# How much of the last output products is done tile by tile at the end of four feed-forward layers

## The reference

```python
# gated layers, D_FF = 2816, each with an RMS norm ahead of it and one behind it
g, u = split(rms_norm(x) @ w_in);  h = (silu(g) * u) @ w_out
x = x + 0.5 * rms_norm(h, gain)
# squared-ReLU layers, 4096 hidden features, layer norm behind them
y = square(relu(h @ w_up)) @ w_down
x = layer_norm(alpha * x + (1 + gate) * y)
```

## Time and profile before

| | us |
|---|---|
| median of 3 runs (lowest to highest) | 1333.25 (1332.56 to 1333.79) |
| profiled execution, its own time | 1337.71 |
| its span, first to last instruction | 1335.9 |
| PE busy | 1248.5 (93%) |
| DVE busy | 967.7 (72%) |
| ACT busy | 613.6 (46%) |
| DMA, mean over the span | 205 GB/s |

### The profile page before, as it was taken

One profiled execution on the slowest core, in us unless ns is written; L12 is line 12 of the kernel. 1 busy time (PEld: TensorE's weight loads), 2 busy tenths in 40 slices (PEclk: granted clock), 3 DMA queues, 4 the chain that ended last, 5 costly groups with the idle time before them and its releaser, 6 DMA issues.

```text
span 1335.9 us, 14591 instructions
## 1 busy us (share of the span) xinstructions
PE 1248.5 (93%) x5776; PEld 1021.0 (76%) x5776; DVE 967.7 (72%) x1318; ACT 613.6 (46%) x799; POOL 92.8 (7%) x136
## 2 busy tenths in 40 slices
PE   5999999999999989999999888999979986899996
PEld 4878778888888868787787676888767764788885
DVE  4998868866566788877776469887768876765555
ACT  5544435545663634343555534443434642643430
POOL 2000220003300000000000000000000000000000
PEclk9999999999999989999999989999989987999998
DMA  9988984545545588894473237787824531456540
GB/s 291 327 292 295 321 278 170 177 158 152 161 146 189 195 291 293 308 312 158 139 266 124 97 126 264 272 296 270 299 95 161 194 103 35 161 192 227 189 157 32
DMA packets 132883, 274.30 MB, mean 205 GB/s; under 512 B 6208, under 2 KB 51472, under 8 KB 132816
## 3 DMA queue, kind: packets, MB, share of 16 engines
q1 hardware_dynamic: 114960, 209.80, 46.5%
q0 software_dynamic: 17792, 63.56, 14.1%
q10 hardware_dynamic: 64, 0.02, 0.0%
HBM read 270.41 MB, written 2.93 MB: 205 GB/s over the span
## 4 chain that ended last, share of the span: by engine, by line
PE 71%; DVE 14%; DMA 6%; ACT 5%; issue 3%; SPq 1%; DVEq 0%; ACTq 0%
PE ps L424 22%; PE ps L426 21%; PE ps L425 21%; DVE lo_w L1214 4%; DMA w_raw<-in_ffn_w_in 4%; PE ps L527 3%; ACT hi_w L872 2%; DVE piece_acc L1393 2%; SPq L324 1%; ACT area L1145 1%; DMA w_raw<-in_mlp_w_down 1%; PE ps L496 1%; DVE area L1714 1%; ACT aux L894 1%; PE ps L660 1%
## 5 line engine op out<-in xcount | busy, mean ns | idle before, releaser
L1214 DVE TENSOR_TENSOR lo_w<-w_raw,hi_w 128x2048 fp32r<-128x2048 f32 x198 | 452.2, 2293 | 180.9 <-ACT hi_w L872 180.6
L872 ACT ACTIVATE hi_w<-w_raw 128x2048 fp32r<-128x2048 f32 x198 | 377.7, 1917 | 241.2 <-DMA w_raw<-in_ffn_w_in 88.1
L424 PE MATMUL ps<-hi_w,xT_hi 128*128 128x512 f32 x1120 | 451.5, 403 | 17.9 <-DVE xT_lo L1235 13.6
L426 PE MATMUL ps<-lo_w,xT_hi 128*128 128x512 f32 x1120 | 441.8, 394 | 0.0
L425 PE MATMUL ps<-hi_w,xT_lo 128*128 128x512 f32 x1120 | 441.6, 394 | 0.0
L424 PEld LDWEIGHTS ps<-hi_w,xT_hi 128*128 128x128 f32 x1120 | 213.8, 191 | 65.5 <-issue 22.4
L426 PEld LDWEIGHTS ps<-lo_w,xT_hi 128*128 128x128 f32 x1120 | 213.5, 191 | 46.5
L425 PEld LDWEIGHTS ps<-hi_w,xT_lo 128*128 128x128 f32 x1120 | 213.9, 191 | 42.4
L424 PE MATMUL ps<-hi_w,hT_hi 128*128 128x512 f32 x464 | 186.6, 402 | 19.5 <-DVE hT_lo L1379 19.3
L426 PE MATMUL ps<-lo_w,hT_hi 128*128 128x512 f32 x464 | 183.8, 396 | 0.0
L425 PE MATMUL ps<-hi_w,hT_lo 128*128 128x512 f32 x464 | 183.6, 396 | 0.0
(11 more groups left out here) (215 smaller groups left out, 884.2 us busy)
## 6 DMA issues: line engine op xcount, KB each, us to landing
w_raw<-in_ffn_w_in SPq DMA_DIRECT2D x88, 512.0 KB
aux<-in_ada_w POOLq DMA_DIRECT2D x32, 1024.0 KB, 7.7
w_raw<-in_mlp_w_up SPq DMA_DIRECT2D x32, 1024.0 KB
w_raw<-in_mlp_w_down SPq DMA_DIRECT2D x32, 1024.0 KB
w_raw<-in_w_mix_in SPq DMA_DIRECT2D x26, 1024.0 KB
w_raw<-in_ffn_w_out SPq DMA_DIRECT2D x22, 1024.0 KB
area<-in_ada_w POOLq DMA_DIRECT2D x16, 1024.0 KB, 7.2
w_raw<-in_moba_w_in SPq DMA_DIRECT2D x12, 1024.0 KB
```

The lines of the kernel that those rows point to most:

```text
L424: pe.matmul(dst, lhs_hi, rhs_hi, start=start, stop=False)
L426: return pe.matmul(dst, lhs_hi, rhs_lo, start=False, stop=stop)
L872: act.activation(hi_w[:, ring_slot(u), :], w_raw[:, ring_slot(u), :], ACT.Copy).then_inc(w_hi, 1)
L1214: vec.tensor_tensor(lo_w[:, ring_slot(u), :], w_raw[:, ring_slot(u), :], hi_w[:, ring_slot(u), :].bitcast(F32), ALU.subtract).then_inc(w_l ...
```

## The change

The end of the gated and of the squared-ReLU layers is changed on TensorE's list alone. Unit A is now done whole, with down_unit, on all four parts, and w_used is raised for it there; down_tail is given B and C only. In the gated layers the transpose of the last block (last_T) still stands behind the first unit of down_tail on (0,0) and (0,1), which is now B. In the squared-ReLU layers the transpose of block 7 stands between the two units of block 6, as before, and A follows it whole. down_tail itself is not edited: with two units it does B on (0,0) and (0,1), last_T, C on (0,0), C on (0,1), B and C on (1,0), B on (1,1), the first transpose, C on (1,1), the second transpose.

```diff
@@ swiglu
                 if sums is not None:
                     quadrant_sums(*sums, 7)
-                down_tail(s, [(u0 + 2 * N_FF + i, ffn_hT[i % 3], 0, b0 + i) for i in range(N_FF - 3, N_FF)],
+                pe.wait_ge(hidT_lo, b0 + N_FF - 2)
+                down_unit(u0 + 3 * N_FF - 3, ffn_hT[(N_FF - 3) % 3], 0, False)
+                down_tail(s, [(u0 + 2 * N_FF + i, ffn_hT[i % 3], 0, b0 + i) for i in range(N_FF - 2, N_FF)],
                           lambda: hidden_T(b0 + N_FF - 1, N_FF - 1, 2), x)
@@ mlp
                     down_unit(u + 2, mlp_hT[i % 2], 0, i == 0)
-                    if i < N_MLP - 2:
-                        down_unit(u + 3, mlp_hT[i % 2], 2, False)
-                hidden_T(b0 + N_MLP - 1, N_MLP - 1, 4)
-                tail = [(N_MLP - 2, 1), (N_MLP - 1, 0), (N_MLP - 1, 1)]
+                    if i == N_MLP - 2:
+                        hidden_T(b + 1, i + 1, 4)
+                    down_unit(u + 3, mlp_hT[i % 2], 2, False)
+                tail = [(N_MLP - 1, 0), (N_MLP - 1, 1)]
                 down_tail(s, [(u0 + 4 * i + 4 + half - (i == N_MLP - 1) * 2, mlp_hT[i % 2], 2 * half, b0 + i) for i, half in tail],
                           lambda: None, None if s == S_MLP2 else zt)
```

## The result

The changed kernel takes 1345.39 us (median of 4 runs, 1344.69 to 1346.08) against 1332.9 us before (4 runs on the same chip, 1331.86 to 1333.79). The ratio is 1.0098 with an interval of 1.0074 to 1.0122: 10 to 16 us slower, where 12.4 us had been forecast.

What follows compares the result with a forecast made beforehand. TensorE is 71% of the chain, so only waits on TensorE, or VectorE at the very end, count. 4.9 + 4.2 - 2.1 + 3.4 + 2.0 = +12.4 us gives 1345.6 us; own range 1343 to 1347, with rivals 1340.5 to 1350.

Steps and rivals of the forecast that it cites:

- FFN1, +4.9: End of FFN1: the last block's output unit and tile 0's norm chain come 5.46 us later, next layer starts +4.9 us.
- FFN2, +4.2: End of FFN2: 0.89 us of wait gets covered, the last block still starts 4.41 us later, next layer's entry +4.2 us.
- MLP1, -2.1: End of MLP1: wait for hT_lo falls to 1.5 us at full clock, tile 0's second part comes sooner, -2.1 us.
- MLP2, +3.4: End of MLP2: VectorE, which finishes the kernel, gets tile 0's first part 18 matmuls later, so the end moves +3.4 us.
- rival 4: The two FFN delays vanish in DMA-bound or chain-bound stretches behind them, leaving +1.3 us, 1334.6; chance 0.06.
- The clock, +2.0: TensorE's granted clock may fall behind the new 2.9 us waits at both FFN ends: +1.0 us each, +2.0 us.
- Rival 1: Clock falls in full for 5.5 us at both FFN ends, 2.7 us each instead of 1.0: +3.5 us, 1349; chance 0.15.
- Early release of A: All four ends: unit A's weights are freed 10 us earlier, so later loads issue sooner; counted 0, bound 0 to -0.5 us.

Runs made afterwards that it cites:

- split_late: Changed kernel with unit next+2's split later on ScalarE and VectorE, at both FFN ends and behind the mixing layer: 1340.51 us, 1.0072 of before.
- the two hidden_first runs: Kernel before with MLP1's last modulation half piece moved behind tile 1's factor on VectorE: 1326.13 us (0.9963); the same plus the change at MLP1's end: 1330.19 us (0.9984).
- the four single changes: Kernel before with the change at one layer end only: FFN1 1338.97 us, FFN2 1336.79 us, MLP1 1329.94 us, MLP2 1336.24 us.
- ffn2_only: Kernel before with the change at the end of FFN2 alone: 1336.79 us, ratio 1.0030.

## Why the prediction was right

- **The total**: 1345.6 forecast, 1345.39 measured, +12.4 against +12.5 us. The agreement to 0.1 us is luck: the terms below are off by more, with the clock and MLP1 erring in opposite directions, and medians of before alone went from 1330.3 to 1333.25.
- **FFN1, +4.9**: measured +4.88, with C 5.44 later (5.46) and the chain through the split shown by split_late. The single waits are printed 0.2 us shorter than worked out (1.50 for 1.75, 2.65 for 2.9), since a wait is counted from a matmul's printed end.
- **FFN2, +4.2**: measured +4.12.
- **MLP1, -2.1**: every wait is where it was forecast, the 4.07 us down to 1.35 (1.5) with the clock at 1.00, the new ones of 1.85 (1.9) and 4.01 (4). The size was read from the one execution with the longest slow stretch (5.5 us); against it -1.93 us is measured, but over the five profiled ends of before the change gives 0.7 to 1.9 us, 1.2 in the mean, and 0.9 by time. The term was over-sized. That the normalised rows, and not TensorE, set this end is shown by the two hidden_first runs.
- **MLP2, +3.4**: measured +3.43.
- **Nothing given back (rival 4)**: the four single changes sum to +12.4 us by time, and the changed kernel's +10 to +16 us leave out the rival's +1.3.
- **The clock, +2.0**: over-sized. Of four waits of 2.6 us at FFN ends (two in the changed kernel, one each in the single ones) one was followed by half the clock, and it cost 0.7 us. The distances of the two profiles explain 11.2 of the 12.5 us, with MLP1 at its mean of -1.2 us 11.9, and what remains is inside the interval of the measurement. Rival 1 (5.5 us of slow clock at both ends) did not come about. The Trainium skill's price for a throttled stretch ("TensorE: Matmul & The Clock Gate", section on HAM oscillation) would make this one fall of 3.4 us cost 1.7 us. As what TensorE itself loses, the traces agree: in split_late, where no wait followed, a fall of 3.4 us cost 1.6. The layer of the changed kernel lost only 0.7, since the entry's wait of 1.06 us (ffn2_only) was filled by slow matmuls.
- **Early release of A**, counted at 0: the waits of TensorE at these ends are all released by hT_lo, x, xT_lo or the normalised rows, none by a weight unit.

## What to carry to other kernels

A tail that finishes output parts one by one has two jobs: to cover the way of the last block's inputs, and to give the first tile's norm a head start. Work moved ahead of it serves the first and robs the second; so first work out which of the two is late at each end, from the start of the first part to the first instruction that needs the norm (here 8.25 us against 5.5 us of cover). Where a wait is set by an in-order queue, look at what stands ahead in that queue before covering the wait with other work: moving a half piece on VectorE gave 4.9 us by time (5.0 to 6.9 in profiles) where cover had given 0.9 (0.7 to 1.9). And where the clock falls in the stretch that is compared, read it from several executions: one profile gave twice the gain that the times show.

## What the runs showed of the hardware that was not expected

Two idle times of TensorE of the same printed length, 2.65 us, in the same execution were followed by a granted clock of 1.00 (214.30 to 218.00) and of 0.50 (656.20 to 659.60). The wait for hT_lo near 80 us lasted 2.27 us in two kernels that are alike up to there, and was followed by 1.00 over 3.4 us in the one (before) and by 0.50 in the other (split_late). One unchanged stretch of some 410 us (mixing and FFN2) took 409.3 to 415.1 us over twelve profiled executions, which is as much as one layer end's change.

How well a single profile's distance can be trusted depends on the end. Over the kernels that leave an end as it was, FFN2's (from L548 to tile 1's transposes) is 25.27 to 25.34 us in nine, and MLP2's 27.91 to 28.04 us in seven. FFN1's (from unit A) is 23.67 to 23.70 us in six of nine but 24.03 to 24.56 in three, and MLP1's, with the half clock in it, 32.83 to 34.72 us in five.
